# One more feed-forward in seven products, and the modulation sums on TensorE: a macaron FNet/HGRN2 diffusion step on one core

## The reference, cut to what matters

```python
mod = (jax.nn.silu(cond) @ w_mod + b_mod)[:, None, :]
sh1, sc1, g1, sh2, sc2, g2, sh3, sc3, g3 = jnp.split(mod, N_MOD, axis=-1)
h = rms_norm(x, norm_pre[0]) * (1.0 + sc1) + sh1
x = x + 0.5 * g1 * rms_norm(swiglu(h, ffn_w_in[0], ffn_w_out[0]), norm_post[0])
h = rms_norm(x, norm_pre[1]) * (1.0 + sc2) + sh2
m, s_f, s_b = mixer(h, ...)          # Fourier mixing and a scan of 4 heads
x = x + g2 * rms_norm(m, norm_post[1])
h = rms_norm(x, norm_pre[2]) * (1.0 + sc3) + sh3
x = x + 0.5 * g3 * rms_norm(swiglu(h, ffn_w_in[1], ffn_w_out[1]), norm_post[2])
```

## Time and profile before

| what | value |
|---|---|
| median of 3 runs | 1442.42 us (1439.97 to 1444.91) |
| the profiled execution's own time | 1442.57 us |
| its span, and mean granted TensorE clock | 1440.0 us, 0.996 |
| TensorE busy | 1404.4 us (98%) |
| DVE busy | 722.6 us (50%) |
| ACT busy | 527.9 us (37%) |
| POOL busy | 658.7 us (46%) |

### The profile page before, as it was taken

How to read it: one execution, slowest core, us unless ns; L and a number is a source line. 1 busy time by engine, 2 the same in 40 slices (tenths; PEclk the granted TensorE clock), 3 DMA queues, 4 the chain that set the end, 5 groups by cost and what they waited for, 6 DMA issues and landing times.

```text
span 1440.0 us, 23202 instructions
## 1 busy us (share of the span) xinstructions
PE 1404.4 (98%) x9661; PEld 1294.8 (90%) x9661; DVE 722.6 (50%) x1067; ACT 527.9 (37%) x791; POOL 658.7 (46%) x507
## 2 busy tenths in 40 slices
PE   6999999999999999999999999999999999989998
PEld 5899999999888888998989999989999999978876
DVE  3388888211001431478777312144677777766043
ACT  6312222222334663233434222266344334345233
POOL 0333433344566682323223433543455565558663
PEclk9999999999999999999999999999999999999999
DMA  9766664222545551212112222413122232235465
GB/s 320 267 211 214 203 235 133 67 80 76 174 129 164 175 198 47 61 52 61 51 40 64 74 73 74 146 59 103 45 74 80 82 88 74 74 89 159 132 184 181
DMA packets 215291, 173.32 MB, mean 120 GB/s; under 512 B 6472, under 2 KB 175636, under 8 KB 215060
## 3 DMA queue, kind: packets, MB, share of 16 engines
q1 hardware_dynamic: 212820, 170.78, 37.7%
q10 hardware_dynamic: 2368, 1.07, 0.3%
HBM read 168.65 MB, written 3.17 MB: 119 GB/s over the span
## 4 chain that ended last, share of the span: by engine, by line
PE 82%; DVE 9%; issue 4%; ACT 2%; DMA 1%; SPq 1%; POOL 0%; DVEq 0%; ACTq 0%
PE PP L612 42%; PE PP L631 8%; PE PP L633 8%; PE PP L632 8%; PE PP L1145 7%; DVE W_lo L2216 2%; DVE S_in L2204 2%; PE PP L656 1%; PE PP L827 1%; PE PP L670 1%; PE PP L951 1%; DMA XTOK<-in_x_sample 1%; DVE TT L2223 1%; PE PP L967 1%; DMA W_in<-in_ffn_w_out 1%
## 5 line engine op out<-in xcount | busy, mean ns | idle before, releaser
L550 POOL TENSOR_TENSOR W_lo<-W_in,W_hi 128x512 fp32r<-128x512 f32 (+1 forms) x380 | 481.0, 1291 | 645.7 <-ACT W_hi L1208 639.1
L1208 ACT ACTIVATE W_hi<-W_in 128x1024 fp32r<-128x1024 f32 x181 | 190.9, 1057 | 445.6 <-PE PP L612 262.5
L612 PE MATMUL PP<-Hhi,W_hi 128*128 128x320 f32 (+2 forms) x1216 | 285.9, 313 | 0.0
L612 PE MATMUL PP<-Hlo,W_hi 128*128 128x320 f32 (+2 forms) x1216 | 280.9, 309 | 0.0
L612 PE MATMUL PP<-Hhi,W_lo 128*128 128x320 f32 (+2 forms) x1216 | 280.8, 309 | 0.0
L612 PEld LDWEIGHTS PP<-Hhi,W_hi 128*128 128x128 f32 x1216 | 202.6, 188 | 9.0 <-issue 6.9
L612 PEld LDWEIGHTS PP<-Hhi,W_lo 128*128 128x128 f32 x1216 | 204.4, 188 | 0.0
L612 PEld LDWEIGHTS PP<-Hlo,W_hi 128*128 128x128 f32 x1216 | 204.4, 188 | 0.0
L559 POOL TENSOR_TENSOR W_lo<-W_in,W_hi 128x512 fp32r<-128x512 f32 x54 | 77.7, 1453 | 99.1 <-DVE W_in L2195 93.0
L1877 DVE SCALAR_TENSOR_TENSOR PP<-modl,S,PP 128x512 f32<-128x512 f32 x144 | 95.8, 744 | 0.0
L631 PE MATMUL PP<-W_hi,Mlo 128*128 128x512 f32 x220 | 86.8, 395 | 4.8 <-DVE Mhi L2233 3.2
(11 more groups left out here) (294 smaller groups left out, 2682.6 us busy)
## 6 DMA issues: line engine op xcount, KB each, us to landing
W_in<-in_ffn_w_out SPq DMA_DIRECT2D x176, 256.0 KB, 3.1
W_in<-in_ffn_w_in SPq DMA_DIRECT2D x83, 512.0 KB, 3.9
modl<-in_w_mod SPq DMA_DIRECT2D x14, 2048.0 KB, 9.2
W_in<-in_w_in SPq DMA_DIRECT2D x32, 512.0 KB, 3.9
modw<-in_w_mod SPq DMA_DIRECT2D x4, 2048.0 KB, 14.2
HL<-g_rows SPq DMA_DIRECT2D x6, 512.0 KB, 5.7
...
```

Source lines behind the costliest of these rows:

```text
L550: return nc.gpsimd.tensor_tensor(lo[:, k0:k1, :], full[:, k0:k1, :], hi[:, k0:k1, :].bitcast(fp32), ALU.subtract)
L612: m = mm(out[:, 0:c1 - c0], w[:, k, :], src[:, c0:c1], start=lead and n == 0 and a == 0, stop=tail and n == len(x) - 1 and a == 2)
L1208: A(W[i][0], W[i][2], ACT.Copy).then_inc(hi_done, 1)
```

## The change

In neutral words: pairs 4 to 21 of the first feed-forward are multiplied with the seven products that `in1` uses (a new stage `in0s`; the four pairs ahead stay whole). All the functions of the seven products now take the number f of the feed-forward. The order of the products, of `last_sum` and of ACT's high parts is altered for both loops. All 14 late modulation slabs go through `mod_slab` on TensorE: four behind slabs 2, 3, 5 and 7, and one behind each of the first ten pairs of `in0s`. They use one buffer (a second one for slab 1 alone), and SP waits with each load for the product of the slab ahead. The hidden values of the first feed-forward are kept whole in `M32` and split behind the pairs as in the second. The eight small loads at the start are issued by ACT. The diagonal copies go from DVE to ACT. Three low parts of `out1B` are made between DVE's additions to x. The diff's core, in four pieces (stages, SP and the modulation's loads; POOL and TensorE; ACT; DVE):

```diff
+SEVENTHS = ("in0s", "in1s")
...
-    ("in0", 2 * FT, [0, 1, 2, 11] + [0, 1, 2] * 14, False),
+    ("in0", 2 * EARLY_PAIRS, [0, 1, 2, 11, 0, 1, 2, 0], False),
+    ("in0s", 2 * SEVEN, [12, 1, 2, 0], False),
...
-MOD_AFTER = [2, 3]
+MOD_AFTER = [2, 3, 5, 7]
...
+        sets = (((4, 2, 0, 3), (5, 2, 1, 3)), ((4, 5, 0, 1), (6, 7, 2, 3)))[f]
+        return [bank(n)[:, 0:HALF] for n in sets[p % 2]]
...
-        sp.dma_start(ident[:, :], t_const).then_inc(sem("const_in"), 16)
-        sp.dma_start(rowsA[0:72, :], b_mod.rearrange("l (r q) -> (l r) q", q=P)).then_inc(sem("rows_in"), 16)
...
         sp.dma_start(XTOK[:, 0, :], x_prompt[0]).then_inc(sem("x_in0"), 16)
...
-            s = i % 2
+            s = int(i == 1)
             sp.dma_start(modl[s][:, :, :], wm[:, :, (MOD_EARLY + i) * 512:(MOD_EARLY + i + 1) * 512])\
...
-        late = 2
-        for n in range(4, 2 * FT):
+        def next_mod(i):
...
+            sp.wait_ge(sem("mod_mm"), MOD_EARLY + (1 if i == 2 else i))
+            load_mod(i)
...
+        for n in (4, 5, 6):
             load_in0(n)
-            while late < MOD_LATE and FREE[n] >= (MOD_AFTER[late - 2] if late < 2 + MOD_PE else 2 * late - 3):
-                if late < 2 + MOD_PE:
-                    sp.wait_ge(sem("mod_mm"), mod_added(late - 2))
-                else:
-                    sp.wait_ge(sem("mod_sum"), late - 1 - MOD_PE)
-                load_mod(late)
-                late += 1
+        next_mod(2)
+        load_in0(7)
+        for p in range(SEVEN):
+            j = EARLY_PAIRS + p
+            load(BASE["in0s"] + 2 * p, 0, KT, w0[:, :, j * P:(j + 1) * P])
+            load(BASE["in0s"] + 2 * p + 1, 0, KT, w0[:, :, DFF + j * P:DFF + (j + 1) * P])
+            if 3 + p < MOD_LATE:
+                next_mod(3 + p)
```

```diff
             low(*(x[:, 0:KH, :] for x in gate)).then_inc(sem("seven_lo"), 1)
             pool.wait_ge(sem("seven_hi"), 7 * p + 4)
+            low(*(x[:, :, :] for x in s1)).then_inc(sem("seven_lo"), 1)
+            pool.wait_ge(sem("seven_hi"), 7 * p + 5)
             low(*(x[:, 0:KH, :] for x in value)).then_inc(sem("seven_lo"), 1)
-            pool.wait_ge(sem("seven_hi"), 7 * p + 5)
...
+        def seven_products(f, p):
+            _, gate, value = seven_slabs(f, p)
+            s1, s2, s4 = S_AT[p]
+            x, y, z, v = seven_banks(f, p)
+            first, second = p == 0, p == 1
+            p += f * SEVEN
...
+            pe.wait_ge(sem("seven_lo"), 5 * p + 1)
...
+            elif not first and not second:
+                pe.wait_ge(sem("hid_a"), p - 1)
+            product(x, quadrant(gate, 0, KH), b11).then_inc(sem("product"), 1)
+            pe.wait_ge(sem("seven_lo_dve"), 2 * p + 1)
...
+            elif not (f and second):
+                pe.wait_ge(sem("u3_done"), back)
+            product(y, s2, T2).then_inc(sem("product"), 1)
+            pe.wait_ge(sem("seven_lo"), 5 * p + 2)
...
+            elif not second:
+                pe.wait_ge(sem("hid_b"), p - 1)
+            product(z, s1, T1).then_inc(sem("product"), 1)
+            pe.wait_ge(sem("seven_lo"), 5 * p + 3)
+            pe.wait_ge(sem("u2_done"), p + 1)
+            if first:
+                pe.wait_ge(sem("t3_lo"), f + 1)
+            product(y, quadrant(value, 0, KH), T3, True).then_inc(sem("product"), 1)
+            pe.wait_ge(sem("seven_lo_dve"), 2 * p + 2)
+            pe.wait_ge(sem("p1_copied"), p + 1)
+            product(x, quadrant(gate, KH, KT), b21, True).then_inc(slab_done, 1)
...
+            elif not (f and second):
+                pe.wait_ge(sem("c21_done"), back)
+            product(v, quadrant(value, KH, KT), T4).then_inc(slab_done, 1)
+            pe.wait_ge(sem("seven_lo"), 5 * p + 5)
+            pe.wait_ge(sem("c22_done"), p + 1)
+            product(z, s4, b22, True).then_inc(sem("product"), 1)
...
+        def late_mod(i):
...
+            mod_slab(modl[int(i == 1)], i, i == 0)
...
-            for i in range(MOD_PE):
...
-                if n == 2 * (i + 2):
-                    pe.wait_ge(sem("mod_sum"), i + 2 - MOD_PE)
-                    for q in range(4):
-                        row = 2 * (i + q // 2) + q % 2
-                        m = mm(PP[3][32 * q:32 * q + 32, 0, :], ONE[:, 30 - row:62 - row],
-                               mod_set(i + q // 2)[q % 2][:, :], start=False, stop=True, skip_group_check=True)
-                    m.then_inc(sem("mod_mm"), 1)
...
+        for p in range(SEVEN):
+            seven_products(0, p)
+            if p <= last_mod:
+                late_mod(len(MOD_AFTER) + p)
+            if p == last_mod + 1:
                 fold_mod(2, modrowl)
```

```diff
-        out_group(0, 1, Mhi, Mlo, None)
+        out_group(0, 0, Mlo, Mhi, ("mid_split", 0))
...
+        act.dma_start(ident[:, :], t_const).then_inc(sem("const_in"), 16)
+        act.dma_start(rowsA[0:72, :], b_mod.rearrange("l (r q) -> (l r) q", q=P)).then_inc(sem("rows_in"), 16)
...
-        act.wait_ge(sem("vec_T"), 2)
-        A(VA[:, :], PP[2][:, 0, 0:120], ACT.Copy).then_inc(sem("vec_evac"), 1)
-        A(VB[:, :], PP[2][:, 1, 0:36], ACT.Copy).then_inc(sem("vec_evac"), 1)
         for t in range(NCH):
+            if t == 2:
+                act.wait_ge(sem("vec_T"), 2)
+                A(VA[:, :], PP[2][:, 0, 0:120], ACT.Copy).then_inc(sem("vec_evac"), 1)
+                A(VB[:, :], PP[2][:, 1, 0:36], ACT.Copy).then_inc(sem("vec_evac"), 1)
...
+        next_hi()
         mod_rows(2, modrow[0])
-        next_hi()
...
+        def seven_gates(f):
...
+            for p in range(SEVEN):
+                i, _, _ = seven_slabs(f, p)
+                x = seven_banks(f, p)[0]
+                n = f * SEVEN + p
+                if p:
+                    second_gate(f, p - 1)
+                    act.wait_ge(sem("u3_done"), n)
+                else:
+                    act.wait_ge(sem("hid_ready"), (1 + 2 * f) * EARLY_PAIRS)
+                act.wait_ge(sem("product"), 5 * n + 1)
+                A(A_P1, x, ACT.Copy).then_inc(sem("p1_copied"), 1)
+                if p + 1 < SEVEN:
+                    gate_highs(f, p + 1)
+                    value_highs(f, p + 1)
+                else:
+                    for j in range(EARLY_PAIRS):
+                        whole_high(f, j)
+                if f == 0:
+                    late_rows(p)
+                act.wait_ge(slab_done, i + 1)
+                A(x, x, ACT.Silu).then_inc(sem("gate_a"), 1)
...
+            second_gate(f, SEVEN - 1)
...
+        def diagonal_blocks(hd):
+            act.wait_ge(sem("at_done"), 7 * hd + 5)
...
+            for q in range(4):
+                part = slice(32 * q, 32 * q + 32)
+                m = A(tiles[part, :, part], ATN[part, :, :], ACT.Copy)
+            m.then_inc(sem("at_diagonal"), 1)
```

```diff
+                    slab_low("out1B", (6, 9, 12)[t])
                     x_add(2, t)
-                for m in (6, 9, 12):
-                    slab_low("out1B", m)
...
+        def last_sum(f, p):
...
+            if p:
+                dve.wait_ge(sem("product"), 5 * (p - 1) + 3)
...
+            V.tensor_tensor(s4[2][:, :, :], gate[2][:, KH:KT, :], s2[2][:, :, :], ALU.subtract)\
+                .then_inc(sem("s_made"), 1)
...
-        def mod_sum(i):
...
+        def seven_sums(f):
...
+            for p in range(SEVEN):
...
+                if p:
+                    c12(f, p - 1)
+                dve.wait_ge(sem("p1_copied"), n + 1)
+                dve.wait_ge(sem("product"), 5 * n + 2)
+                if n:
...
+                V.tensor_tensor(A_U2, A_P1, y, ALU.add).then_inc(sem("u2_done"), 1)
+                if p:
+                    hidden_b(f, p - 1)
+                if p + 1 < SEVEN:
+                    first_sums(f, p + 1)
+                    last_sum(f, p + 1)
+                else:
+                    whole_low(f, 0)
+                dve.wait_ge(sem("product"), 5 * n + 4)
+                if n:
+                    dve.wait_ge(sem("c21_done"), n)
...
+                V.tensor_tensor(A_U3, A_P1, y, ALU.add).then_inc(sem("u3_done"), 1)
...
+                V.tensor_tensor(A_C22, A_U3, z, ALU.add).then_inc(sem("c22_done"), 1)
+                if p + 1 < SEVEN:
+                    lows(f, p + 1)
+                else:
+                    whole_low(f, 1)
+                    whole_low(f, 2)
+                dve.wait_ge(slab_done, i + 2)
...
+                V.tensor_tensor(A_C21, A_U3, v, ALU.subtract).then_inc(sem("c21_done"), 1)
+                dve.wait_ge(sem("gate_a"), n + 1)
+                dve.wait_ge(sem("c21_done"), n + 1)
+                V.tensor_tensor(M32[:, EARLY_PAIRS + p, 0:HALF], x, A_C21, ALU.mult).then_inc(sem("hid_a"), 1)
+                if f == 0 and p == MOD_LATE - len(MOD_AFTER) + 1:
+                    late_vectors()
```

More of the change, by code:

```diff
@@ L125, in plan @@
         free[base["in1A"] + n] = after
-    free[base["in1"]] = base["in1A"] - 1
+    free[base["in0s"]] = 4
+    free[base["in1s"]] = base["in1A"] - 1
     return base, buf, free, order, need, fresh
```

(77 more changed lines are left out.)

534 lines of the change are left out of this document (207 added, 327 removed).

## The result

The changed kernel took 1405.94 us in the median (1405.32 to 1409.35, 4 executions) against 1441.52 for the kernel before, executed beside it: a ratio of 0.9755, 95% interval 0.9731 to 0.9779, so 35.6 us or 2.5% faster. The forecast was 1404.5, the range 1399 to 1419. The profiled execution took 1406.2 us with a span of 1404.3; the spans differ by 35.7.

What follows compares the result with a forecast made beforehand. TensorE was taken to bound the kernel, with PE at 98%, plus some pieces of 3 to 11 us. The terms summed to −37.9 us from the profiled 1442.57, giving 1404.7, or 1404.5 by the median; range 1399 to 1419.

Steps and rivals of the forecast that it cites:

- the second loop's and the heads' terms: Second loop: pairs fall from 12.97 to 12.31 us, −11.2; heads: four diagonal copies leave DVE, ending KD waits, −3.3.
- the rival on the other side: First feed-forward: the single buffer makes modulation loads late in ten pairs, 1450 us, slower than before; chance 0.03.
- The products: First feed-forward: seven products shorten 18 pairs from 14.18 to 12.31 us, TensorE taken as the bound, −33.6.
- The modulation: First feed-forward: twelve more slabs on TensorE at 1.85 us, six final sums of 1.00 fewer, +16.2.
- The late vectors: Inside the first loop: some 12 small operations now run on DVE, 2.2 us against its slack, +0.9.
- The borders: Loop to output stage: about 1 us idle at both, no half clock; `in1` −3.8, `in0` +1.3.
- The end: Last output side: three lows between additions take half of the 1.6 us wait for W_lo, −0.8.
- the start: Kernel's start: eight issues moved to ACT −3.1, Avec −1.0, slab 1's later lows +0.5; sum −3.6.
- the Avec step: Start: an Avec operation took 1.21 us against 0.17 elsewhere, blamed on POOL's lows beside it, which now wait; −1.0.
- DVE's slack: Seven-product loops: DVE and ACT's round stays 0.8 us a pair below TensorE's 12.31.
- The sum of 11.5 us: Loops, per pair: 7.44 us on DVE and ACT, four operations of 0.49 and three first sums of 0.69.
- The rival that the vectors stay the bound: Both loops: DVE meeting POOL's lows keeps the period at 12.97 us; 1421 us, partially 1415 to 1421; chance 0.14.

Runs made afterwards that it cites:

- old order's run: Changed kernel with the old order of products, last_sum, ACT's value highs and POOL's value low put back in both seven-product loops; 1426.39 us.
- late-loads run: Changed kernel with SP waiting for product 4 of the running pair before each modulation load from the fifth on; 1451.23 us.
- border's run: Changed kernel with whole highs and lows of the first pairs put back behind the loop at both borders to the output stage; 1419.24 us.

## Why the prediction was right, and where it was off

**Right by mechanism:** a pair is 84 matmuls at TensorE's pace in both loops (12.32 forecast 12.31); the second loop's and the heads' terms came within 1 us; the modulation's loads were hidden with 4 us to spare; the time lies 1.4 us above the forecast, the gain 2.2 below it. The old order's run shows that the orders are needed, and the late-loads run that the rival on the other side was a real one.

**Mis-sized terms.** *The products:* the step took 14.18 for a whole pair from the chain, but that stretch holds the switch to the sums; five whole pairs behind one another took 70.48 us, 14.10 each. So 18 × 1.78 = −32.0 instead of −33.6. *The modulation:* priced at 1.85 a slab; with the switch it is 2.05, and a pair's sums cost 1.16 (two whole pairs with one took 139.13 − 109.78 = 29.35 us): 24.6 − 7.0 = +17.6 instead of +16.2. *The late vectors:* one wait of 0.5 us for U2 instead of +0.9. *The borders:* `in0`'s got an idle of 0.66 where 1.0 was forecast, `in1`'s too; but the output side behind the first is 1.2 longer, most of it by a new wait of 0.8 for Mhi inside it (the waits for W_lo there, 0.6, were there before). *The end:* −3.9 instead of −2.4; with 1.7 of it the clock by the border's run, PE's three waits for W_lo there (1.6 with one for DVE's) went whole, not by half. The rest of it was not traced, and no run put the three lows back.

**The step that failed: the start.** −3.1 was put on issues moved from SP to ACT; undone, they cost 0.2. The x tiles came earlier, but x was no longer what PE waited for: the fillers (56 instead of 52) began at 9.94 instead of 5.55, behind the small loads, which now landed later, and reached to 18.4, some 3 us beyond ACT's first scaled tile. Of the 1.8 us that were gained, 0.9 is the early modulation's earlier start (23.95 → 23.01), and 1.5 lies between it and the first product (10.47 → 8.93 us), where the Avec step was: Avec's two operations take 0.36 now instead of 1.90. That term, −1.0, was undersized. 0.7 was lost again behind the first product, where slab 1's lows came later (forecast 0.5).

**Mis-sized on the safe side: DVE's slack.** The sum of 11.5 us took last_sum and the first low at the lengths that they had beside POOL, 1.4 us more than they take in the new order, and it put silu and the copy of P1, which ACT does beside DVE, into the same round. DVE's busy time in the second loop's window is 147.83 / 18 = 8.2 us a pair, and it has 3 us to spare. The rival that the vectors stay the bound was therefore further off than its chance of 0.14 said. The Trainium skill (SBUF — State Buffer, section Who interferes with whom) has it that DVE instructions with two SBUF inputs contend with GpSimd's reads; the trace agrees in the loop (last_sum takes 0.69 us in the changed kernel and 1.66 behind C22, beside POOL's lows), and the last section shows how far it can go.
